# Chunk 6 split ahead of helper work in `up`, `gu0` and `gu1`, and five modulation pieces moved to later chunks

## What is computed

```python
h = rmsnorm(x, ffn_pre_norm)                                   # first block
u = causal_depthwise_conv(h @ w_up, conv_w, conv_b)            # w_up: 1024 x 5632
gate, up = jnp.split(u, 2, axis=-1)
x = x + rmsnorm((gelu(gate) * up) @ w_down, ffn_post_norm)     # w_down: 2816 x 1024

for layer in range(2):                                         # second block
    m = silu(c) @ ada_w[layer] + ada_b[layer]                  # ada_w: 1024 x 6144
    shift_m, scale_m, gate_m, shift_f, scale_f, gate_f = jnp.split(m[:, None, :], 6, axis=-1)
    h = rms_norm(x, norm_gains[layer, 0]) * (1 + scale_m) + shift_m
    x = x + gate_m * mixer(h)                                  # attention, retention
    h = rms_norm(x, norm_gains[layer, 1]) * (1 + scale_f) + shift_f
    gt, up = jnp.split(h @ w_gate_up[layer], 2, axis=-1)       # 1024 x 5632
    x = x + gate_f * ((silu(gt) * up) @ w_down[layer])         # 2816 x 1024
return rms_norm(x, final_norm)
```

## Time and profile before

| | us |
|---|---|
| median of 3 runs | 1041.67 (1041.29 to 1041.73) |
| profiled execution | 1041.22 |
| its span | 1039.4 |
| TensorE busy | 1020.3 (98%) |
| VectorE busy | 812.4 (78%) |
| ScalarE busy | 594.4 (57%) |
| GpSimd busy | 162.5 (16%) |

### The profile page before, as it was taken

One profiled execution on the slowest core, in us unless ns is written; L12 is line 12 of the kernel. 1 busy time (PEld: TensorE's weight loads), 2 busy tenths in 40 slices (PEclk: granted clock), 3 DMA queues, 4 the chain that ended last, 5 costly groups with the idle time before them and its releaser, 6 DMA issues.

```text
span 1039.4 us, 18373 instructions
## 1 busy us (share of the span) xinstructions
PE 1020.3 (98%) x7424; PEld 953.2 (92%) x7424; DVE 812.4 (78%) x1397; ACT 594.4 (57%) x1029; POOL 162.5 (16%) x167
## 2 busy tenths in 40 slices
PE   8999999999999999999999999999999999999997
PEld 8888898999889997999999889988999899999887
DVE  5778799999997977588999798885668676674553
ACT  6688676666446766665444455544465566544443
POOL 0000134333102100032212011201100123111010
PEclk9999999999999999999999999999999999999999
DMA  9833356777893433457998787553434536774441
GB/s 359 312 117 123 122 196 245 289 277 255 344 398 144 154 128 117 193 191 271 381 370 308 282 319 279 203 182 142 162 123 170 195 131 234 278 270 152 168 167 41
DMA packets 34609, 228.49 MB, mean 220 GB/s; under 512 B 3803, under 2 KB 4075, under 8 KB 10972
## 3 DMA queue, kind: packets, MB, share of 16 engines
q1 hardware_dynamic: 33884, 224.69, 57.8%
q0 software_dynamic: 640, 2.62, 0.6%
HBM read 224.68 MB, written 2.62 MB: 219 GB/s over the span
## 4 chain that ended last, share of the span: by engine, by line
PE 84%; DVE 9%; ACT 3%; DMA 2%; issue 1%; POOL 0%; POOLq 0%; SPq 0%; DVEq 0%; ACTq 0%
PE psum L1523 16%; PE psum L1524 15%; PE psum L1525 15%; PE psum L1567 9%; PE psum L1568 5%; DVE w_lo L2300 3%; PE psum L1592 2%; PE psum L1595 2%; PE psum L1594 2%; PE psum L1964 2%; PE psum L1966 2%; PE psum L1965 2%; DMA raw<-in_w_in 2%; ACT w_hi L825 1%; PE psum L1755 1%; DVE arena L2632 1%
## 5 line engine op out<-in xcount | busy, mean ns | idle before, releaser
L2300 DVE TENSOR_TENSOR w_lo<-raw,w_hi 128x1024 fp32r<-128x1024 f32 (+2 forms) x340 | 387.2, 1160 | 134.9 <-ACT w_hi L825 129.4
L825 ACT ACTIVATE w_hi<-raw 128x1024 fp32r<-128x1024 f32 (+2 forms) x340 | 334.3, 997 | 215.7 <-PE psum L1525 84.6
L1523 PE MATMUL psum<-h_hi,w_hi 128*128 128x256 f32 (+1 forms) x1128 | 319.6, 283 | 5.4 <-DVE w_lo L2300 3.1
L1524 PE MATMUL psum<-h_hi,w_lo 128*128 128x256 f32 (+1 forms) x1128 | 316.7, 281 | 0.0
L1525 PE MATMUL psum<-h_lo,w_hi 128*128 128x256 f32 (+1 forms) x1128 | 316.4, 280 | 0.0
L1523 PEld LDWEIGHTS psum<-h_hi,w_hi 128*128 128x128 f32 x1128 | 212.4, 188 | 8.6 <-DVE w_lo L2300 5.2
L1525 PEld LDWEIGHTS psum<-h_lo,w_hi 128*128 128x128 f32 x1128 | 212.3, 188 | 0.0
L1524 PEld LDWEIGHTS psum<-h_hi,w_lo 128*128 128x128 f32 x1128 | 211.6, 188 | 0.7 <-issue 0.7
L1523 PE MATMUL psum<-hid,w_hi 128*128 128x256 f32 (+1 forms) x532 | 152.8, 287 | 0.5 <-DVE w_lo L2300 0.4
L1525 PE MATMUL psum<-hid,w_hi 128*128 128x256 f32 (+1 forms) x532 | 150.0, 282 | 0.0
L1524 PE MATMUL psum<-hid,w_lo 128*128 128x256 f32 (+1 forms) x532 | 150.0, 282 | 0.0
(11 more groups left out here) (316 smaller groups left out, 1386.9 us busy)
## 6 DMA issues: line engine op xcount, KB each, us to landing
arena<-in_ada SPq DMA_DIRECT2D x48, 1024.0 KB, 6.9
raw<-in_gu SPq DMA_DIRECT2D x44, 1024.0 KB, 6.8
raw<-in_ret_in SPq DMA_DIRECT2D x24, 1024.0 KB, 4.8
raw<-in_up SPq DMA_DIRECT2D x22, 1024.0 KB, 4.8
raw<-in_dn SPq DMA_DIRECT2D x32, 704.0 KB, 4.2
raw<-in_qkv SPq DMA_DIRECT2D x12, 1024.0 KB, 5.0
raw<-in_down SPq DMA_DIRECT2D x11, 1024.0 KB, 8.4
raw<-in_ret_o SPq DMA_DIRECT2D x8, 1024.0 KB, 4.8
```

Source lines behind the costliest of these rows:

```text
L825: nc.scalar.activation(w_hi[chunk % SPLIT_SLOTS][:, a:b], raw[chunk % RAW_SLOTS][:, a:b], ACT.Copy)\
L1523: nc.tensor.matmul(out, w[0], hc, start=start, stop=False, skip_group_check=True)
L1524: nc.tensor.matmul(out, w[1], hc, start=False, stop=False, skip_group_check=True)
L2300: tt(w_lo[s][:, a:b], raw[chunk % RAW_SLOTS][:, a:b], w_hi[s][:, a:b].bitcast(F32), ALU.subtract)\
```

## The change

Three things are changed. The split of chunk 6 of `up`, `gu0` and `gu1` is taken out of the loop and stands right after the settled chunk 2, on ScalarE ahead of that chunk's rounding (in `up`, of the rounding of chunk 1's product), on VectorE ahead of the first step of the loop; in `gu0` and `gu1` VectorE's split of chunk 5 also stands ahead of three waits instead of behind them. `unit_free` no longer counts a chunk in a spare bank: chunks 7 and 8 wait for the read-out of chunks 3 and 4, which had their banks, instead of chunks 5 and 6. And pieces move: in `up` from chunk 7 to chunk 20 (pieces now at 9, 11, 13, 15, 17, 19, 20, 21), from `gu0`'s chunks 4 to 7 to `dn0`'s chunks 2, 6, 10 and 14 (`gu0` now at 8 to 19, `dn0` at each chunk but 0, 4, 8, 12). The number of pieces, 48, stays.

```diff
--- before.py
+++ after.py
@@ -115,8 +115,8 @@
 
 
 ADA_PIECES = 24
-ADA_STEPS = [("w_in", 10, lambda c: int(c in (KA, QA0))), ("up", 22, lambda c: int(c >= 7 and c % 2)),
-             ("down", 11, lambda c: int(c < 10)), ("gu0", 22, lambda c: int(4 <= c <= 19)), ("dn0", 16, lambda c: c % 2),
+ADA_STEPS = [("w_in", 10, lambda c: int(c in (KA, QA0))), ("up", 22, lambda c: int(c >= 9 and c % 2 or c == 20)),
+             ("down", 11, lambda c: int(c < 10)), ("gu0", 22, lambda c: int(8 <= c <= 19)), ("dn0", 16, lambda c: int(c % 4 > 0)),
              ("gu1", 22, lambda c: int(10 <= c <= 13))]
 
 ADA_LATE = 2
@@ -407,8 +407,10 @@
 
         def unit_free(eng, ph, step, f):
 
-            if ph.unit0 + f(step.j) >= 2:
-                eng.wait_ge(lin_free[(ph.unit0 + f(step.j)) % 2], step.n(lambda c: (ph.unit0 + f(c)) // 2))
+            u = f(step.j)
+            if ph.unit0 + u >= 2:
+                skipped = int(spare(ph, u - 2))
+                eng.wait_ge(lin_free[(ph.unit0 + u) % 2], (ph.unit0 + u) // 2 - skipped)
 
         def leave(ins, unit):
             return ins.then_inc(lin_free[unit % 2], 1)
@@ -1210,13 +1212,14 @@
             round_hid(Step(2), 2)
             gelu(Step(3))
             conv_settled(2)
+            hi(ph.chunk0 + 6)
             round_hid(Step(3), 2)
 
             def up_step(step):
                 c = step.j
                 if step.i is None and c < 4:
                     return
-                if c < ph.n and (step.i is not None or c > 4):
+                if c < ph.n and (step.i is not None or c > 5):
                     hi(ph.chunk0 + c + 1, step if step.i is not None else None, ph)
                 if c <= ph.n:
                     conv_start(step)
@@ -1385,7 +1388,7 @@
                     if ph.name == "gu1" and step.j == 9:
                         act.wait_ge(cond_in, 32)
                         nc.scalar.activation(cond_silu, cond_silu, ACT.Silu).then_inc(cond_ready, 1)
-                    if step.i is not None or step.j > 4:
+                    if step.i is not None or step.j > 5:
                         hi(ph.chunk0 + step.j + 1, step if step.i is not None else None, ph)
                     silu(step)
                     round_hid(step, 1, ph.unit0)
@@ -2708,6 +2712,7 @@
             taps_settled(1)
             lo(ph.chunk0 + 5)
             taps_settled(2)
+            lo(ph.chunk0 + 6)
             steps(dve, ph.n, 8, 1, up_step)
             up_step(Step(ph.n))
             lo(PH["down"].chunk0 + 1)
@@ -2898,13 +2903,14 @@
                         pieces(ph.name, step)
 
                 for c in range(DEFERRED_CHUNKS):
+                    if c == 2:
+                        lo(ph.chunk0 + 5)
                     dve.wait_ge(gelu_ready, base + c + 1)
                     dve.wait_ge(settled, 2 * DEFERRED_CHUNKS * deferred_before(i) + 2 * c + 2)
                     dve.wait_ge(hid_tiles, base + c - 1)
-                    if c == 2:
-                        lo(ph.chunk0 + 5)
                     cut = slice(S * (c % 2), S * (c % 2) + S)
                     stt(ff["hid"][:, cut], settled_tile(i, c, 1), shift_sum(i, c, 1), ff["g"][:, cut], ALU.add, ALU.mult).then_inc(first_products, 1)
+                lo(ph.chunk0 + 6)
                 steps(dve, ph.n, 14 if ph.name == "gu1" else 8, 2, one)
                 one(Step(ph.n))
 
```

## The result

| | before | after |
|---|---|---|
| median (lowest to highest) | 1041.67 (1041.29 to 1041.73, 4 runs) | 1053.55 (1052.20 to 1054.28, 4 runs) |
| profiled execution, span | 1041.22, 1039.4 | 1052.20, 1050.4 |
| VectorE busy | 812.4 | 815.3 |
| ratio after to before | | 1.0126 [1.0109, 1.0144] |

The changed kernel is 11.9 us slower. The sign and the two places of the loss were forecast; the forecast change was +4.2, so the size was not, and the time lies above the range (1040.5 to 1049.0). The page, beside the earlier trace rows: the chain that ended last has 3 points more on VectorE and 2 more on transfers.

A forecast was written before the change was run, and what follows sets the result against it. TensorE, busy 1020.3 of 1039.4 us, was taken to bound the kernel. The terms -4.9 + 3.0 + 6.1 = +4.2 us on the median 1041.67 gave 1045.9, range 1040.5 to 1049.0.

The forecast's parts named there:

- The four early waits: TensorE's waits at chunks 6 and 7 of `up` and `gu0` were to go: 4.9 us gained.
- `up`'s piece: Piece moved to `up`'s chunk 20 delays the splits of `down`'s first chunks: 3.0 us lost, between 1.5 and 3.6.
- Inside `dn0`: The added pieces were to make TensorE late by some 0.9 us at `dn0`'s chunks 12 and 13.
- the group of 16.5 us: VectorE's work for four chunks of `dn0`, about 16.5 us against 15.4 of TensorE's, with 2.49 us a piece.
- `ret_in`'s first matmul: Starts late behind `dn0`'s last piece, by VectorE's backlog (4.6 us) or the transfers (5.7): 4.8 us in the sum.
- After it: In `ret_in`, VectorE's chain lags about 1 us more than TensorE, some of which shows: 0.4 us lost.
- (c): Rival, 15%: TensorE's clock falls in the idle of nearly 5 us before `ret_in`, costing 1.7 us: 1047.6.
- (d): Rival, 4%: transfers are the limit in `dn0`, weights late in each group by 1 to 1.5 us more: 1049 to 1050.
- (a): Rival, 10%: the late pieces are hidden and only the four waits in `up` and `gu0` go: 1036.8.
- (b): Rival, 20%: the ends of `up` and `dn0` cost only VectorE's part, transfers landing at the fastest seen: 1042.7.
- (e): Rival, 4%: ScalarE or chunk 4's slot holds the early split, so its gain is halved: 1048.4.
- (f): Rival, 5%: matmul spacing changes; `gu0` at the faster one would give 2.0 us over some 19 chunks.

The follow-up runs named there:

- e3: Kernel before with only the four pieces moved from `gu0`'s chunks 4 to 7 to `dn0`: 1048.78 us, ratio 1.0071.
- e1: Kernel before with the early split of chunk 6 and the looser bank count, all pieces left in place: 1041.72 us, ratio 0.9993.
- e8: Kernel before with the looser bank count alone: 1041.36 us, ratio 1.0003.
- e6: Changed kernel with the last piece's request of `up` and `dn0` behind the next stage's first three weight loads: 1052.36 us, ratio 1.0115.
- e7: Changed kernel with the piece of `dn0`'s chunk 14 back at `gu0`'s chunk 7: 1048.73 us, ratio 1.0077.
- e12: e11 plus the unused matmuls of e4 ahead of the waits in `down` and `ret_in`: 1053.65 us, ratio 1.0121.
- e4: Changed kernel with matmuls on unused data, 25 before the bank wait in `down` and 34 before `ret_in`: 1051.81 us, ratio 1.0097.
- e2: Kernel before with only `up`'s piece moved from chunk 7 to chunk 20: 1046.70 us, ratio 1.0051.
- e5: Kernel before with early split, looser bank count, and `up`'s piece of chunk 7 moved to `down`'s chunk 6: 1038.33 us, ratio 0.9977.
- e10: Kernel before with 16 matmuls on unused data ahead of the first scores at 38 us: 1042.57 us, ratio 1.0010.
- e11: Changed kernel with 16 matmuls on unused data ahead of the first scores at 38 us: 1054.61 us, ratio 1.0136.

## Why the prediction was wrong

- **The four early waits, -4.9.** Right, and in size (-4.8). But its reasons were shared wrongly: in `gu0` the pieces alone do it (e3), and in `up` the split and the bank count alone only move the wait to chunk 9 (e1, e8). That chunk 9's bank would come "within 0.1 us of being late" was right as far as it went, with the piece gone.
- **`up`'s piece, +3.0 for 5.0.** The step that failed is the consumer. The backlog was right: the 3.6 us of "taps of 20, piece 21, taps of 21" are there. But the prediction asked only when `down`'s splits come, and overlooked that chunk 0 of `down` needs in its middle a bank that the last taps free, with 1.3 us of room in before. The wait was 3.2, near the upper bound of 3.6, and the clock fell at its end (+1.2), which was priced at nothing. e6 shows that the order on the queue, which the prediction called hidden "by a hair", is more than half of the loss.
- **Inside `dn0`, +0.9 for 2.7.** The step that failed is the group of 16.5 us: 2.49 us a piece was the fastest row, one that no GpSimd instruction lies beside. The group measured 17.42. Over the stage's three groups the difference (2 to 3 us) is the missing 1.8 here and what VectorE is later at the last piece (640.65 for 638.2).
- **`ret_in`'s first matmul, +4.8 for 4.9.** The mechanism is right, with both bounds near each other as described; that the size fits is partly luck. Both bounds came 2 to 2.6 us later than computed (the piece's end at 643.2 for 640.6, the transfer at 642.8 for 640.7), and the wait kept its size because TensorE, held up in `dn0`, came 1.8 later too. e7 shows that both go with one piece less. Of the two the transfer, with the rounding behind it, is the later, by 0.6 in after and by 1.9 in e12.
- **After it, +0.4 for 2.7.** The step that failed is "some of which shows". VectorE's chain to the norm's factor is 0.8 us later than the first matmul at its start and 1.6 at its end, and TensorE has nothing to do meanwhile, so all of it shows and more. Some 0.8 of the 2.7 goes when the clock stays up (e4).
- **Rivals.** (c), the clock's fall before `ret_in`, came true on top of the forecast, and at `down` too; its mechanism is right and its price there too high (1.7 for the 0.5 of e4 and nothing in e12), because a late VectorE covers it. It should have stood in the forecast, not beside it: an idle time of nearly 5 us was already part of the sum. (d) did not: no wait in `dn0` goes to a transfer. The windows above moved 423 GB/s, so the 358 of the Trainium skill (DMA: Bandwidth & Descriptors, "Where 436 GB/s comes from") is no limit for one core alone here, and the trace disagrees with that rule. (a), (b) and (e) are out by the waits of after. (f) did not happen in after but did in e1, e2, e5 and e10.
- **Left over.** The median of after lies 1.35 above its profiled run, before's 0.45; that 0.9 of the 11.9 no single trace explains.

Open: what sets the spacing of 5.65 or 5.76 us; what makes the kernels reach `up` 4.2 us apart; what the low clock costs at `ret_in`; and why the low clock lasted 3.4 us in some places and 6.8 in others.

## What to carry to other kernels

Work moved off a stage's start to the last chunks of a stage lands where the engine's queue must also feed the next stage: list every consumer of what is queued behind it (splits, banks, transfers, the norm), not only the next one, and price it with rows that overlap what it will overlap. Where the sum itself contains an idle time of TensorE near 3 us or longer, put a fall of the clock into the sum, and then ask whether another engine's chain covers it. And a wait on a bank that is only loosened comes back two chunks later; less work on the engine that frees the bank is what removes it.

## What the runs showed of the hardware

- After the first 35 us the clock fell to its lower level at each of nine idle times of TensorE of 2.7 us or more (2.7 in e1, 3.0 in after, e2, e7 and e11, 4.2 in e3, 4.3 in e11, 4.4 in after, 6.7 in e6), at four of the six of 2.4 to 2.5 us at 38 us (e1, e3, e4 and e12, not after and e10), and at none of 1.6 us (e7), 1.7 (e5, e6) and 2.2 (before). At the start it fell at one of 1.2 us in before and in after, so the length of the idle time alone does not decide. The Trainium skill (TensorE: Matmul & The Clock Gate, "Why this matters for your kernels") warns that gaps between bursts bring the lower clock back; the traces agree. The price was 0.36 us per microsecond of low clock at `down`, where TensorE led (e4, e12).
- A multiply-reduce of 1024 columns on VectorE takes 1.22 us alone and up to 1.75 beside a GpSimd instruction: in after none of the 49 with no GpSimd row at the time took over 1.3, of the 47 others 27 did. The Trainium skill (SBUF — State Buffer, "Who interferes with whom") says that a VectorE instruction with two inputs in SBUF contends with a GpSimd instruction that reads SBUF; the trace agrees, at 0.2 to 0.5 us for each.
- Matmuls of 256 columns on the fp32r tiles keep one of two spacings for tens of microseconds (427 or 419 in 50 us), at a granted clock of 1.00 in both; in `gu0` it changed only at waits of 0.2 to 1.2 us (e1, e2, e5, e8, e10).
